# Post-norm weights multiplied in ahead of the factor, and the first FFN chunk's gate and up run together by operand chunk

## The reference, cut to what matters

```python
def _rmsnorm(x, g, eps=RMS_EPS):
    xf = x.astype(jnp.float32)
    y = xf * lax.rsqrt(jnp.mean(xf * xf, axis=-1, keepdims=True) + eps)
    return (y * g.astype(jnp.float32)).astype(x.dtype)

def _half_ffn(x, g_pre, g_post, w_gate, w_up, w_down):
    h = _rmsnorm(x, g_pre)
    f = (jax.nn.silu(h @ w_gate) * (h @ w_up)) @ w_down
    return x + 0.5 * _rmsnorm(f, g_post)
...
        x = _half_ffn(x, ...)                    # FFN 3 / FFN 5, post-norm 0 / 3
        h = _rmsnorm(x, mix_norm_pre[i])
        m = _conformer_conv(h, ...)  or  _diff_attention(h, ...)
        x = x + _rmsnorm(m, mix_norm_post[i])    # post-norm 1 / 4
        x = _half_ffn(x, ...)                    # FFN 4 / FFN 6, post-norm 2 / 5
```

## Time and profile before

| | us |
|---|---|
| median of 3 runs (1897.39 to 1898.2) | 1897.88 |
| the profiled execution | 1898.13 |
| its span, first to last instruction | 1896.3 |
| TensorE busy | 1732.7 (91%) |
| TensorE weight loads busy | 1593.8 (84%) |
| VectorE busy | 1227.8 (65%) |
| ScalarE busy | 817.1 (43%) |
| GpSimd busy | 39.3 (2%) |
| mean granted clock of TensorE | 0.959 |

### The profile page before, as it was taken

One profiled execution on the slowest core, in us unless ns is written; L12 is line 12 of the kernel. 1 busy time (PEld: TensorE's weight loads), 2 busy tenths in 40 slices (PEclk: granted clock), 3 DMA queues, 4 the chain that ended last, 5 costly groups with the idle time before them and its releaser, 6 DMA issues.

```text
span 1896.3 us, 29255 instructions
## 1 busy us (share of the span) xinstructions
PE 1732.7 (91%) x11365; PEld 1593.8 (84%) x11365; DVE 1227.8 (65%) x1737; ACT 817.1 (43%) x1199; POOL 39.3 (2%) x23
## 2 busy tenths in 40 slices
PE   7869999997697999999989869999899989689997
PEld 7857799996577999899988769998899989589997
DVE  4778566666767666656668856665766654866665
ACT  4556454335444333533442054434443344744433
POOL 0000000000005000000000000000000000000000
PEclk9979999999799999999989989999999989889999
DMA  7610345453224554454534035554455545035553
GB/s 265 210 45 1 100 168 198 177 188 112 88 70 144 186 190 175 167 193 173 198 126 152 1 111 187 189 187 178 150 194 185 180 144 167 1 101 209 190 189 143
DMA packets 53291, 285.93 MB, mean 151 GB/s; under 512 B 5872, under 2 KB 6128, under 8 KB 30704
## 3 DMA queue, kind: packets, MB, share of 16 engines
q1 hardware_dynamic: 52224, 281.46, 41.5%
q0 software_dynamic: 1008, 3.67, 0.6%
HBM read 284.05 MB, written 1.05 MB: 150 GB/s over the span
## 4 chain that ended last, share of the span: by engine, by line
PE 81%; DVE 12%; ACT 5%; issue 2%; DMA 0%; SPq 0%; DVEq 0%; ACTq 0%
PE bank L812 18%; PE bank L814 18%; PE bank L813 18%; PE bank L955 9%; PE bank L923 3%; PE bank L925 3%; PE bank L927 3%; DVE proj L1684 3%; PE bank L826 2%; PE bank L1012 1%; PE bank L971 1%; ACT whi L428 1%; PE bank L992 1%; DVE att L1416 1%; DVE nmax L1418 1%
## 5 line engine op out<-in xcount | busy, mean ns | idle before, releaser
L812 PE MATMUL bank<-hthi,whi 128*128 128x256 f32 x2240 | 638.6, 285 | 2.7 <-DVE wlo L1242 1.8
L813 PE MATMUL bank<-htlo,whi 128*128 128x256 f32 x2240 | 635.6, 284 | 0.0
L814 PE MATMUL bank<-hthi,wlo 128*128 128x256 f32 x2240 | 635.5, 284 | 0.0
L1236 DVE TENSOR_TENSOR wlo<-raw,whi 128x2048 fp32r<-128x2048 f32 x175 | 401.2, 2292 | 102.7 <-ACT whi L428 102.6
L812 PEld LDWEIGHTS bank<-hthi,whi 128*128 128x128 f32 x2240 | 431.7, 193 | 9.5 <-DVE htlo L1296 2.6
L813 PEld LDWEIGHTS bank<-htlo,whi 128*128 128x128 f32 x2240 | 431.5, 193 | 4.7
L814 PEld LDWEIGHTS bank<-hthi,wlo 128*128 128x128 f32 x2240 | 431.3, 193 | 0.0
L428 ACT ACTIVATE whi<-raw 128x2048 fp32r<-128x2048 f32 x175 | 333.9, 1908 | 24.3 <-PE bank L814 17.2
L499 ACT ACTIVATE tr<-tr 128x256 f32<-128x256 f32 x132 | 55.1, 418 | 657.1 <-DVE tr L1312 657.1
L1312 DVE TENSOR_TENSOR tr<-bank,rb 128x512 f32<-128x512 f32 x132 | 91.2, 691 | 234.0 <-PE bank L814 234.0
L1242 DVE TENSOR_TENSOR wlo<-raw,whi 128x1024 fp32r<-128x1024 f32 x174 | 213.1, 1225 | 27.3 <-ACT whi L436 26.5
(11 more groups left out here) (236 smaller groups left out, 1945.0 us busy)
## 6 DMA issues: line engine op xcount, KB each, us to landing
raw<-in_stream SPq DMA_DIRECT2D x176, 1024.0 KB, 5.5
raw<-in_stream SPq DMA_DIRECT2D x176, 512.0 KB, 3.6
wide<-in_wide POOLq DMA_DIRECT2D x7, 512.0 KB, 4.0
x<-in_x SPq DMA_DIRECT2D x1, 1024.0 KB, 5.2
out<-x SPq DMA_DIRECT2D x2, 512.0 KB, 2.8
wide<-in_const SPq DMA_DIRECT2D x1, 960.0 KB, 15.4
const<-in_const SPq DMA_DIRECT2D x1, 897.0 KB, 12.6
cols<-in_cols SPq DMA_DIRECT2D x1, 340.0 KB, 7.6
```

The source lines that it names most:

```text
L812: nc.tensor.matmul(out, whi_, mhi, start=start, stop=False)
L813: nc.tensor.matmul(out, whi_, mlo, start=False, stop=False)
L814: return nc.tensor.matmul(out, wlo_, mhi, start=False, stop=stop)
L1236: V.tensor_tensor(wlo[:, s, 0:UA], raw[:, s, 0:UA], whi[:, s, 0:UA].bitcast(F32), ALU.subtract)\
```

## The change: what it does

- **Post-norm.** The weights (and the 0.5 of an FFN) are multiplied into `xn` before the factor is there: after an FFN straight behind ScalarE's square of the same bank, behind a mixer after each step. With the factor VectorE makes one pass, x = xn * factor + x. The first half of x comes in two pieces of 256 columns; the second half (512 columns) is put behind the first htlo pair of the next operand. In the last post-norm both halves follow at once. TensorE waits per round of transposes, where it waited per half. ScalarE's squares go to unused parts of `proj`, as `xn` is in use. `s_wu` is gone, and GpSimd's row loads wait for `s_fg`, which counts the finished products.
- **First chunk of an FFN.** `gate_up_first` works both halves of a chunk k before it goes on to k+1: per k six matmuls, three to each half of the bank. `norm_rows` moves into the middle of chunk 1's gate half.
- **Order on ScalarE and VectorE.** `hi_a` of the next unit is issued ahead of the operand (FFN 1, 2, 3), ahead of `post_ffn` (FFN 5) or in the mixer's last step ahead of the square root's table (FFN 4, 6). On VectorE `lo_b` moves ahead of the copy of `rb`.

```diff
+POST_PIECES = [4, 3, 4, 4, 3, 4]
+POST_BASE = [sum(POST_PIECES[:k]) for k in range(6)]
+AFTER_POST = (5, 6, 7, 8, 9)
...
+                if n == 3:
+                    pool.wait_ge(s_evd, plan[U_PW2 + 2][3])
+                elif n >= 2:
+                    k = {2: 0, 4: 1, 5: 2, 6: 3}[n]
+                    pool.wait_ge(s_fg, POST_BASE[k] + POST_PIECES[k])
...
 # ScalarE, ffn chunk
-                    hi_a(f + j + 1, i)
                     if first:
                         norm(m)
+                    else:
+                        hi_a(f + j + 1, i)
                     hi_b(f + j, i)
...
 # ScalarE, mixer_out
                     hi_a(u + 1)
                     if w == 2:
+                        hi_a(u + 2)
                         sqrt_table()
...
 # ScalarE, main order (also U_F1 and U_F2)
+            hi_a(U_F3 + 1)
             operand("op_f3", [(c, col("ffn_pre", c)) for c in range(DC)], U_F3)
...
+            hi_a(U_F5 + 1)
             post_ffn(2, U_F4)
...
 # TensorE, x_operand
                 def there(q):
+                    if m in AFTER_POST:
+                        pe.wait_ge(s_x, 4 * m - 3 + (0, 1, 3, 3)[q])
+                    elif q % 2 == 0:
+                        pe.wait_ge(s_x, 4 * m - 2 + q) if m else pe.wait_ge(s_ldx, 16)
...
+            def gate_up_first(f, ready):
+                s = f % 2
+                pe.wait_ge(s_loa, f + 1)
+                for k in range(DC):
+                    ready(k)
+                    for half in range(2):
+                        out, at = gub[0][:, half * T:(half + 1) * T], half * 1024 + k * P
+                        nc.tensor.matmul(out, whi[:, s, at:at + P], hthi[:, k, :], start=k == half == 0, stop=False,
+                                         skip_group_check=True)
...
+                ins.then_inc(s_usea, 1)
...
 # TensorE, ffn
-                gate_up(f, 0, ready=x_operand(f"op_f{fi + 1}", m))
-                norm_rows(f"r_f{fi + 1}", m)
-                gate_up(f, 1)
+                gate_up_first(f, x_operand(f"op_f{fi + 1}", m))
+                gate_up(f, 1, halfway=lambda: norm_rows(f"r_f{fi + 1}", m))
...
 # VectorE, operand
+                    if a == 2 and after_first is not None:
+                        after_first()
...
 # VectorE, ffn chunk
                     if first:
-                        norm_rows(f"r_f{fi + 1}", m)
+                        rstd(f"n{m}", 2, at=NORM)
                     lo_b(f + j, i)
+                    if first:
+                        copied_rows(f"r_f{fi + 1}")
...
 # VectorE, post_ffn
+                def gained(n_):
+                    t, j = n_ % 2, n_ // 2
+                    sl = slice(j * 512, (j + 1) * 512)
+                    V.scalar_tensor_tensor(out=xn[:, t, sl], in0=acc[2 * t + j][:, :], scalar=0.5, in1=wide[:, row % 2, sl],
+                                           op0=ALU.mult, op1=ALU.mult).then_inc(s_fg, 1)
+
+                dve.wait_ge(s_ldw[row % 2], 16 * (row // 2 + 1))
+                for n_ in range(3):
+                    dve.wait_ge(s_pss, done + n_ + 1)
+                    gained(n_)
+                dve.wait_ge(s_pss, done + 4)
                 V.tensor_tensor(ss[:, 0:2], ...).then_inc(s_phs, 1)
+                gained(3)
                 rstd(f"post{k}", 2)
...
+            def add_scaled(t, sl):
+                return V.scalar_tensor_tensor(out=x[:, t, sl], in0=xn[:, t, sl], scalar=rs[:, t:t + 1], in1=x[:, t, sl],
+                                              op0=ALU.mult, op1=ALU.add)
+
+            def add_first_half(k):
+                for q in range(2):
+                    dve.wait_ge(s_fg, POST_BASE[k] + (q + 1 if POST_PIECES[k] == 3 else 2))
                     for t in range(NT):
+                        ins = add_scaled(t, slice(q * 256, (q + 1) * 256))
+                    ins.then_inc(s_x, 1)
+
+            def add_second_half(k):
+                dve.wait_ge(s_fg, POST_BASE[k] + POST_PIECES[k])
+                for t in range(NT):
+                    add_scaled(t, slice(512, 1024)).then_inc(s_x, 1)
...
-            operand("op_f4", [(c, col("ffn_pre", 8 + c)) for c in range(DC)])
+            operand("op_f4", [(c, col("ffn_pre", 8 + c)) for c in range(DC)], lambda: add_second_half(1))
...
 # VectorE, main order: the lambda products move behind the operand of QKV
```

More of the change, by code:

```diff
@@ L286, in build @@
         sg = tr[:, 0:512].rearrange("p (c n) -> p c n", c=2)
+        junk = [proj[:, 2304 + i * PITCH:2304 + (i + 1) * PITCH] for i in range(6)]
+        junk_ffn = [proj[:, i * 512:(i + 1) * 512] for i in range(4)]
         hidf = tr[:, 512:1024].rearrange("p (c n) -> p c n", c=2)
@@ L900, in step, with gate_up @@
                 ins.then_inc(s_useb, 1)
-            def gate_up(f, c, i=0, ready=None):
+            def gate_up_first(f, ready):
[7 more added lines that the diff above has]
+                                         skip_group_check=True)
+                        nc.tensor.matmul(out, whi[:, s, at:at + P], htlo[:, k, :], start=False, stop=False,
+                                         skip_group_check=True)
+                        ins = nc.tensor.matmul(out, wlo[:, s, at:at + P], hthi[:, k, :], start=False, stop=k == DC - 1,
+                                               skip_group_check=True)
+                ins.then_inc(s_usea, 1)
+            def gate_up(f, c, i=0, halfway=None):
                 s, b = (f + c) % 2, c % 2
@@ L907, in gate_up @@
                     for k in range(DC):
-                        if ready is not None and half == 0:
-                            ready(k)
+                        if halfway is not None and half == 0 and k == DC // 2:
+                            halfway()
                         at = half * 1024 + k * P
@@ L1288, in norm_rows, with operand @@
                 dve.wait_ge(s_tf[r % 2], r // 2 + 1)
-            def operand(name, chunks):
+            def operand(name, chunks, after_first=None):
                 for a in range(0, len(chunks), 2):
                     r = RD[name] + a // 2
+                    if a == 2 and after_first is not None:
+                        after_first()
                     dve.wait_ge(s_thi, OPN[name] + a // 2 + 1)
@@ L1346, in post_ffn @@
+                dve.wait_ge(s_fg, POST_BASE[k] + 4)
                 for j in range(2):
-                    sl = slice(j * 512, (j + 1) * 512)
                     for t in range(NT):
-                        ins = V.scalar_tensor_tensor(out=xn[:, t, sl], in0=acc[2 * t + j][:, :], scalar=rs[:, t:t + 1],
-                                                     in1=wide[:, row % 2, sl], op0=ALU.mult, op1=ALU.mult)
-                    if j == 0:
-                        own(ins)
-                    else:
-                        ins.then_inc(s_wu, 1)
-                        dve.wait_ge(s_wu, row + 1)
@@ new lines, in mixer_out, with gained @@
+            def mixer_out(first, k, row, bias=None):
+                def gained(w):
+                    u = first + w
+                    sl = slice(w * PITCH, w * PITCH + STEPS[u][2][0][1])
+                    dve.wait_ge(s_ldw[row % 2], 16 * (row // 2 + 1))
+                    dve.wait_ge(s_evd, plan[u][3])
+                    for t in range(NT):
+                        ins = V.tensor_tensor(xn[:, t, sl], m_out[:, t, sl], wide[:, row % 2, sl], ALU.mult)
+                    ins.then_inc(s_fg, 1)
@@ L1375, in mixer_out @@
                     ins.then_inc(s_evd, 1)
-            def post_mixer(k, row, first):
+                    gained(w)
                 dve.wait_ge(s_eva, plan[first + 2][2])
@@ L1381, in post_mixer @@
                 rstd(f"post{k}", 2)
-                dve.wait_ge(s_ldw[row % 2], 16 * (row // 2 + 1))
-                for j in range(2):
-                    sl = slice(j * 512, (j + 1) * 512)
-                    for t in range(NT):
-                        ins = V.scalar_tensor_tensor(out=xn[:, t, sl], in0=m_out[:, t, sl], scalar=rs[:, t:t + 1],
-                                                     in1=wide[:, row % 2, sl], op0=ALU.mult, op1=ALU.mult)
-                        if k == 1 and j == t == 0:
-                            ins.then_inc(s_wu, 1)
-                    if j == 0:
-                        own(ins)
-                    else:
-                        ins.then_inc(s_wu, 1)
-                        dve.wait_ge(s_wu, row + 1)
-                    for t in range(NT):
-                        V.tensor_tensor(x[:, t, sl], x[:, t, sl], xn[:, t, sl], ALU.add).then_inc(s_x, 1)
+                add_first_half(k)
             def attention(kind):
@@ L1671, in _ @@
             post_ffn(0, 0)
+            operand("op_conv", [(c, col("mix_pre", c)) for c in range(DC)], lambda: add_second_half(0))
             V.memset(conv_u[:, :, 0:PAD], 0.0)
             V.memset(conv_u[:, :, PAD + T:], 0.0)
-            operand("op_conv", [(c, col("mix_pre", c)) for c in range(DC)])
             def conv_taps(chunks_, k0, k1, ready=None):
@@ L1746, in _ @@
```

(6 more changed lines are left out.)

40 lines of the change are left out of this document (20 added, 20 removed).

## The result

The changed kernel takes 1884.96 us (median of 4 executions, 1882.76 to 1888.43) against 1897.83 us for the kernel before (1897.39 to 1898.20). The ratio is 0.9921, 95% interval 0.9895 to 0.9948: 15.0 us faster by the ratio, 12.9 by the medians, where 8.6 were forecast. In the three later series 40 of the 50 executions of the kernel before took 1896.3 to 1902.1 us and 10 took 1911.8 to 1912.6, none of which was profiled, and as such executions make a gain look larger in a ratio, the medians are the safer figure. Two more series gave medians of 1886.28 (ratio 0.9941, 0.9928 to 0.9954) and 1887.16 us (0.9915, 0.9883 to 0.9948). Over all 16 executions the median is 1886.6, and they spread over 6.4 us. The three executions of the kernel before that the forecast started from spread over 0.8 us, which was too small a sample.

The account below looks back on a forecast made before the run. TensorE, carrying 81% of the chain of waits, was taken as the bound, so only its standstills could be shortened. Terms 1.8 + 0 + 1.8 + 0.75 + 0.1 - 0.1 + 1.15 + 1.05 + 2.15 = 8.7 us gave 1889.3 us, range 1884.5 to 1894.

Parts of the forecast that it names:

- FFN 1 and 3 start, 1.8 each: First chunk of FFN 1 and FFN 3, both halves together: first down product 1.8 us earlier in each.
- FFN 2, 0: FFN 2's first chunk: paced by GpSimd's five diagonal instructions, so 0 us gained and TensorE's 7.58 us wait grows.
- Tail, 2.15: Tail behind post-norm 5: adds end earlier and the stores follow 1.3 us apart instead of 2.6, gaining 2.15 us.
- Shape of the post-norm: Post-norm starts: transposes 1.4 us earlier, third rounds only 0.75 to 1.15, VectorE's second half of x late next.
- Two accumulations in one bank: Rival, interleaved FFN chunks: switching between halves of one bank slows 288 matmuls, priced at +26 us, 1915 us; chance 0.05.
- Second half eats all: Rival, post-norm starts: VectorE's second half of x takes the whole first gain, starts give 0, 1892.4 us; chance 0.08.
- Early copies cost nothing: Rival, ScalarE's early operand copies: they find ScalarE free, 1.95 us back, 1886.5 us; chance 0.10.
- Less 1.0: Post-norm 2, start of FFN 5: ScalarE's early weight copy makes the squares 1.0 us later, net about -0.1 us.
- FFN 4, 5, 6 ... I take 0: First chunks of FFN 4, 5, 6, starting at 1.2 GHz: bounds +0.2 to -0.8 us, taken as 0.
- Then 1.22 us to hthi: Post-norm after an FFN: ScalarE's hthi starts 1.22 us after the first transposes, as in the earlier trace.
- the forecast 0.1: Start of FFN 4 (post-norm 1): 1.05 us gained, 0.95 us lost to the early copy, 0.1 us left.
- the first rival: Rival, the five post-norm starts: the clock comes back later, some 3 us at three or four, 1893 us; chance 0.13.

Follow-up runs that it names:

- the two experiments that move it: Changed kernel with GpSimd's diagonal products each waiting for a later hidden chunk of FFN 2: 1883.03 us in five pieces, 1876.26 us in eighteen.
- the chunk part alone: Kernel before plus only the interleaved first FFN chunk, halfway rows and early ScalarE copies, post-norms as before: 1892.07 us, ratio 0.9970.
- the post-norm part alone: Kernel before plus only the post-norm edit, first chunk and operand copies as before: 1891.21 us, ratio 0.9968.
- The pair of displaced kernels: 8 idle products ahead of FFN 1's last down product, added to the changed kernel (1888.60 us) and to the kernel before (1899.96 us).
- the filled waits: Changed kernel with TensorE's idle time in the five post-norms filled by idle 128x128 products: 1878.31 us, ratio 0.9875.

## Why the prediction was right and where it failed

- *FFN 1 and 3 start, 1.8 each:* right (1.76, 1.75), with the margin of hidlo as counted (ready at 248.2, needed at 249.01). *FFN 2, 0:* right, and its cause, GpSimd's work, is shown by the two experiments that move it: without it the first down product comes 9.5 us sooner.
- *Tail, 2.15:* 2.3. *Shape of the post-norm* (transposes first, second half of x late next): right. The wait that I named as next (the second half of x) was worth 4 us, and one line removes it.
- *Two accumulations in one bank:* refuted, products follow after 0.12 us. *Second half eats all:* refuted. *Early copies cost nothing:* refuted for FFN 4 (0.89), half true for FFN 5, true for FFN 6.
- *"Less 1.0" for FFN 5's copy:* mis-sized. The copy costs 0.55, since the squares, once late, find the banks that they read finished and follow each other after 0.57 us instead of 0.69.
- *"FFN 4, 5, 6 ... I take 0":* mis-sized. With the chunk part alone the interleaving gives 0.7 and 0.8 us behind the first transposes of FFN 4 and 5; less their copies (0.9 and 0.4) that is -0.2 and 0.4. In FFN 6 it loses 0.2.
- *The step that failed: "Then 1.22 us to hthi", and with it the clock of before at the five starts.* The 1.22 us of the earlier trace rows were measured with the first transposes behind the clock's fall, at 1.2 GHz. The shorter chain brings them forward, and at four of the five starts of the changed kernel (convolution, FFN 5, QKV, FFN 6) they run before the fall: hthi follows after 0.76 us, and the third round 0.46 us sooner than counted, 1.8 us in all. At the fifth, FFN 4, they come 1.7 us behind the fall, and there the forecast 0.1 was right to the third round (0.13). The terms of the other four were together 2.6 us too small (5.4 against 2.85): these 1.8, the copy of FFN 5 (0.45), and 0.2 at each post-norm after an FFN, where the first transposes gained 1.62 us and not 1.44; some of it was lost again behind the third round.
- *With the post-norm part alone* only FFN 6's first transposes run ahead of the fall. Its gains at the third rounds are 0.91, 1.02, 0.76, 1.13 and 1.48 us; the forecast's terms, without the copies, are 0.75, 1.05, 0.85, 1.15 and 1.05. So the count was sound to 0.2 us wherever its clock was met. What follows the third round it left out: three of the starts lose another 0.3 to 0.5 us there.
- *The clock* was the first rival's matter too, with the wrong sign: at the convolution, FFN 5, QKV and FFN 6 it was low for 6.8 us in the changed kernel, and for 10.2, 6.8, 10.2 and 10.2 in the kernel before.
- *The sum itself* took stages with untouched code at nothing. K and V gave back 1.4 to 1.8 in all three profiles, so that little or nothing was left of FFN 1's gain, and the convolution gave 3.6 in one of three. The pair of displaced kernels shows for K and V that a displacement does it without the change. For the convolution only the two forms are shown; what decides between them in an execution was not found, nor why the changed kernel reaches FFN 1 up to 2.2 us sooner in one execution than in another. How far the time fell below the forecast (4.3 us by the first median, 2.7 by that of all 16 executions) is therefore in part chance: the form of the convolution alone moves an execution by 3.4.

## What to carry to other kernels

A stage's gain is not yet the kernel's: follow the shift through the untouched stages behind it, and when TensorE waits there and its clock changes near the wait, put a range on them. Before you carry a delay over from a row of the kernel before, look at which clock it was measured. To tell a lost gain from a displaced one, add idle work as long as the gain and look whether the loss goes. Where an engine's wait is followed by a slow start, filling the wait with idle products can be worth as much as shortening it (8.3 us by the medians here, and 6.5 for the post-norm part), and a GpSimd instruction beside VectorE should be shorter than VectorE's idle time in a loop turn (1.5 us against about 2 here).

## What the hardware showed that I had not expected

- Displacing the same instructions by 1.7 us switched a stretch at 1.2 GHz on in one kernel and off in another (1.5 us in K and V each time). TensorE had waited 2.9 us just ahead of it in both cases, and as long in the two kernels without the stretch, so the wait alone does not decide it.
- With the first transposes of a start over 1 us ahead of the clock's fall ScalarE's hthi starts 0.75 us behind them, with them behind it 1.21 us, in all 12 profiles without a fill at the starts, the kernel before among them.
- The convolution's 394 products, whose code is the same in all 14 profiles, took 94.0 us in three, 97.3 to 97.7 in nine, 96.1 in one (the chunk part alone) and 98.3 in one (the filled waits). The mean granted clock was 0.95 with 94.0 us, and 0.91 with 97.3 and 97.5. The Trainium skill, "TensorE: Matmul & The Clock Gate", Part 1, says that the number of slow matmuls at the start of one and the same kernel differs between runs. The traces here show a difference of this kind in the middle of a kernel.
- Idle 128x128 products kept the clock at 2.4 GHz through waits of 3 to 5 us. At the start of the convolution 11 of them took 2.62 us and the first transposes came no later.
